# The last strip of a mixture of experts: output rows stored whole, the strip put over them by an indirect store

## The reference

```python
    combine = jnp.einsum('nk,nke->ne', top_w, jax.nn.one_hot(expert_id, N_EXPERTS, dtype=jnp.float32)).astype(xf.dtype)
    y = jnp.zeros_like(xf)
    for e in range(N_EXPERTS):
        h = jax.nn.silu(xf @ w_gate[e]) * (xf @ w_up[e])
        y = y + combine[:, e:e + 1] * (h @ w_down[e])
```

## Time and profile before

| | |
|---|---|
| median of 3 runs | 1213.24 us (1210.46 to 1216.31) |
| the profiled execution | time 1210.47 us, span of its records 1208.6 us |
| mean granted clock of TensorE | 0.978 of full speed |
| TensorE busy | 94% of the span (5834 products) |
| VectorE, ScalarE, POOL busy | 39%, 15%, 4% |
| moved by DMA | 327.6 MB, 271 GB/s over the span |
| chain that ended last | TensorE 80%, VectorE 9%, DMA 6%, ScalarE 4% |

### The profile page before, as it was taken

How to read it: one execution, slowest core, us unless ns; L and a number is a source line. 1 busy time by engine, 2 the same in 40 slices (tenths; PEclk the granted TensorE clock), 3 DMA queues, 4 the chain that set the end, 5 groups by cost and what they waited for, 6 DMA issues and landing times.

```text
span 1208.6 us, 14025 instructions
## 1 busy us (share of the span) xinstructions
PE 1131.5 (94%) x5834; PEld 555.5 (46%) x5834; DVE 471.1 (39%) x966; ACT 186.6 (15%) x401; POOL 48.8 (4%) x63
## 2 busy tenths in 40 slices
PE   7999999999999999999999999999999999959985
PEld 4334343344444455677777673333333333333332
DVE  5000069199565654011123465233333333412332
ACT  2103123200231243000022431000000000000010
POOL 0002000100000012100000001000000000000000
PEclk9999999999999999999999999899999999979998
DMA  8835623655342348854445739999999999999995
GB/s 294 289 129 131 184 86 124 226 174 174 105 137 91 124 184 336 290 145 139 139 158 218 283 116 406 397 415 426 428 426 427 427 425 429 425 427 427 426 427 227
DMA packets 71084, 327.60 MB, mean 271 GB/s; under 512 B 14006, under 2 KB 17878, under 8 KB 54444
## 3 DMA queue, kind: packets, MB, share of 16 engines
q1 hardware_dynamic: 55152, 282.65, 59.8%
q0 software_dynamic: 7888, 37.06, 8.1%
q10 hardware_dynamic: 7980, 6.99, 2.4%
HBM read 318.45 MB, written 10.49 MB: 272 GB/s over the span
## 4 chain that ended last, share of the span: by engine, by line
PE 80%; DVE 9%; DMA 6%; ACT 4%; issue 1%; DVEq 0%; POOL 0%; SPq 0%; ACTq 0%
PE PS L715 21%; PE PS L1042 16%; PE PS L1320 13%; PE PS L1402 7%; DMA ring<-in_w_up 5%; PE PS L1281 4%; PE PS L688 3%; PE PS L1327 2%; DVE X L2087 2%; DVE top L2086 2%; PE PS L1379 1%; PE PS L1285 1%; PE PS L1395 1%; PE PS L709 1%; DMA X<-in_x_prompt 1%
## 5 line engine op out<-in xcount | busy, mean ns | idle before, releaser
L715 PE MATMUL PS<-ring,NC 128*128 128x512 f32 x704 | 320.8, 600 | 1.8 <-issue 1.8
L715 PEld LDWEIGHTS PS<-ring,NC 128*128 128x128 f32 x704 | 128.7, 191 | 153.6 <-issue 152.0
L1042 PE MATMUL PS<-NC,ring 128*128 128x288 f32 x768 | 189.9, 407 | 1.6 <-DVE X L2244 0.5
L1320 PE MATMUL PS<-ring,NC 128*64 128x512 f32 x560 | 163.7, 605 | 7.4 <-DMA ring<-in_w_up 6.8
L1042 PEld LDWEIGHTS PS<-NC,ring 128*128 128x128 f32 x768 | 144.6, 190 | 42.4 <-issue 1.2
L2437 DVE TENSOR_TENSOR X<-X,PS 128x1024 f32<-128x1024 f32 x52 | 63.5, 1221 | 118.9 <-PE PS L1281 118.9
L1320 PEld LDWEIGHTS PS<-ring,NC 128*64 128x64 f32 x560 | 46.3, 138 | 101.3 <-issue 99.9
L1281 PE MATMUL PS<-XNN,NC 64*128 64x512 f32 x208 | 59.1, 645 | 1.4 <-DVE XNN L2475 0.8
L2244 DVE TENSOR_TENSOR X<-X,PS 128x288 f32<-128x288 f32 x16 | 7.3, 455 | 112.0 <-PE PS L1042 112.0
L1931 ACT ACTIVATE NC<-PS,small 64x512 f32<-64x512 f32 x11 | 7.5, 681 | 273.5 <-PE PS L1320 239.7
L1327 PE MATMUL PS<-ring,NC 128*32 128x256 f32 x384 | 36.0, 451 | 14.7 <-DMA ring<-in_w_up 14.7
(11 more groups left out here) (460 smaller groups left out, 1174.0 us busy)
## 6 DMA issues: line engine op xcount, KB each, us to landing
ring<-in_w_gate SPq DMA_DIRECT2D x27, 2048.0 KB, 19.7
ring<-in_w_up SPq DMA_DIRECT2D x22, 2048.0 KB, 17.1
ring<-in_w_in SPq DMA_DIRECT2D x36, 1024.0 KB, 5.1
ring<-in_w_down SPq DMA_DIRECT2D x16, 2048.0 KB, 18.6
ring<-in_w_out SPq DMA_DIRECT2D x16, 1024.0 KB, 5.1
nine<-in_w_down SPq DMA_DIRECT2D x6, 2048.0 KB, 22.0
XNN<-in_w_up SPq DMA_DIRECT2D x5, 2048.0 KB
NC<-in_w_gate SPq DMA_DIRECT2D x5, 2048.0 KB
```

Source lines behind the costliest of these rows:

```text
L715: last = mm(acc(n, t)[:, 0:width], lhs[:, kt, t * 128:(t + 1) * 128], slot(m)[:, k, 0:width], start=kt == 0, stop=kt == KT - 1)
L1042: last = mm(PS[:, j, 0:NT], slot(m)[:, k, 128 * j:128 * j + 128], src[:, kt, :], start=kt == 0, stop=kt == width * 4 - 1)
L1320: last = mm(PS[64 * half:64 * half + 64, 2, :], x[:, kt % 8, kt // 8, :], weights[half][:, kt % 8, :], start=kt == 0, stop=kt == KT - 1)
```

## The change

The last block is combined earlier and the last strip takes another way.

- The combine of block 13 now stands in the gate and up products of expert 15 (`COMBINED_IN`), with strip 0 alone; the rows of strip 1 in `ysb` are cleared by VectorE first. All five steps stand there, and VectorE does their adds before it scales the last hidden. After them, `hx` lacks nothing but the last strip.
- VectorE then signals `rows_final`, and SP stores `hx` as three stores of whole rows.
- TensorE gathers the strip's 32 rows from `hx` by a one-hot matrix `last_hot` (12 products, `last_base`) into bank 5, and the last down product is accumulated on top of them. For this the routing weight is multiplied into the scale of the last hidden.
- VectorE and ScalarE copy the bank into `last_rows`, one instruction each, and POOL writes it over the stored rows by two indirect DMAs, one for the prompt and one for the sample rows, in pieces of 512 columns; rows that belong to the other output are out of bounds and left out. POOL waits for the three stores first.
- The indices and `last_hot` are made by VectorE in the routing.
- The overflow loops of SP, ScalarE and VectorE stand inside `If(nov > 0)`.

```diff
@@ -106,6 +106,7 @@
     put("half", ((p >= 64) + 2 * EMPTY).astype(np.float32))
+    put("quad", (p // 32 + 4 * EMPTY).astype(np.float32))
@@ -410,13 +411,17 @@
         rnk, s32, l32, later = (small[:, 352 + 16 * i:368 + 16 * i] for i in range(4))
         strips = small[:, 416:424].rearrange("p (s b) -> p s b", s=2)
         over_rs = small[:, 490:491]
+        last_tab, last_at, last_out = small[:, 424:427], small[:, 428:429], small[:, 430:431]
+        last_hots = natS[:, 64:256].rearrange("p (i t r) -> p i t r", i=2, t=3)
+        last_hot = last_hots[:, 0, :, :]
+        last_rows = XN[:, 0:512]
+        ids_prompt, ids_sample = ids[:, 114:115], ids[:, 115:116]
         iota_t = gh[:, 0:NT]
         slot_w = C_[:, 3840:3840 + 2 * NT].rearrange("p (b t) -> p b t", b=2)
         NCOMB, NCOMB_OV = 5, 6
         KEYS_WITH_Q = 9
         TOKENS = (0, 128, NT - 128)
         ROW0 = NBK * CAP
-        LAST = [(t, x) for t in range(3) for x in range(2)]
         def sub_of(p):
@@ -438,7 +443,7 @@
             return XT2 if b == BSTAR + 1 else XT
         COMBINED_IN = {p: p - 1 for p in range(1, NFULL)}
-        COMBINED_IN.update({PSTAR: BSTAR - 1, PSTAR + 1: BSTAR, PSTAR + 2: BSTAR + 1})
+        COMBINED_IN.update({PSTAR: BSTAR - 1, PSTAR + 1: BSTAR, PSTAR + 2: BSTAR + 1, NEXP - 1: NBK - 1})
         ids_nov, ids_exp = ids[0:1, 90:91], ids[0:1, 91:91 + NOVF]
         ids_order = ids[0:1, 16:32]
         ids_slot, ids_blk = ids[:, 80:86], ids[:, 108:114]
@@ -454,7 +459,7 @@
         HELD = [(NLOT - 2 + i) % NRING for i in range(2)]
         SPARE = [i for i in range(NRING) if i not in HELD][:NL]
         FREED = NLOT + NRING - 2
-        NCOMB_IN = NCOMB * (NBK - 1)
+        NCOMB_IN = NCOMB * NBK
         r_at = [0]
@@ -558,19 +563,18 @@
             sp.wait_ge(S("route_ready"), 1)
             nov = sp.value_load(ids_nov, min_val=0, max_val=NOVF)
             sp.wait_ge(S("moe_free"), FREED)
-            with sp.Fori(0, NOVF) as b:
...
-            for n, (t, x) in enumerate(LAST):
-                sp.wait_ge(S("y_ready"), n + 1)
-                y, row = (y_prompt, t * 128) if t < 2 else (y_sample, 0)
-                sp.dma_start(bass.AP(y.tensor, row * D + 512 * x, [[D, ROWS[t]], [1024, 2], [1, 512]]),
-                             hx[0:ROWS[t], t, :].rearrange("p (h x c) -> p h x c", h=2, x=2)[:, :, x, :])\
-                    .then_inc(S("y_stored"), 16)
-            sp.wait_ge(S("y_stored"), 16 * len(LAST))
+            with sp.If(nov > 0):
+                with sp.Fori(0, NOVF) as b:
...
+            sp.wait_ge(S("rows_final"), 1)
+            for t in range(3):
+                y = y_prompt[0, t * 128:(t + 1) * 128, :] if t < 2 else y_sample.rearrange("b s d -> (b s) d")
+                sp.dma_start(y, hx[0:ROWS[t], t, :]).then_inc(S("y_stored"), 16)
+            sp.wait_ge(S("y_stored"), 48)
         @block.gpsimd
@@ -644,6 +648,14 @@
                 with pool.If(nov > b):
                     pool.wait_ge(S("xt_ready"), NBK + b)
                     block_rows(NBK + b, 1, "ov_x")
+            pool.wait_ge(S("last_ids"), 1)
+            pool.wait_ge(S("y_stored"), 48)
+            pool.wait_ge(S("last_rows"), 2)
+            for y, at, rows in ((y_prompt[0].rearrange("t (c n) -> (t c) n", c=4), ids_prompt, 4 * T),
+                                (y_sample.rearrange("b s (c n) -> (b s c) n", c=4), ids_sample, 4 * R)):
+                nc.gpsimd.indirect_dma_start(y, bass.IndirectOffsetOnAxis(ap=at, axis=0), last_rows, None,
+                                             bounds_check=rows - 1, oob_is_err=False).then_inc(S("y_put"), 16)
+            pool.wait_ge(S("y_put"), 32)
         @block.tensor
         def _(pe):
@@ -1293,11 +1305,21 @@
                         pe.wait_ge(S("y_out_psum"), k + 1)
                     elif k == BSTAR:
                         pe.wait_ge(S("y_out_psum"), NFULL)
+                    elif k < NBK - 1:
+                        pe.wait_ge(S("y_strips"), 4 * (k - NFULL + 2 - (k > BSTAR)))
                     else:
-                        pe.wait_ge(S("y_strips"), 4 * (k - NFULL + 2 - (k > BSTAR)))
+                        pe.wait_ge(S("y_strips"), 2 * NLIGHT)
                 if NCOMB * k + s:
                     pe.wait_ge(S("comb_free"), NCOMB * k + s)
                 combine(k % 2, s, 6).then_inc(S("comb"), 1)
+
+            def last_base():
+
+                pe.wait_ge(S("last_ids"), 1)
+                for t in range(3):
+                    for c in range(4):
+                        mm(PS[32 * c:32 * c + 32, 5, :], last_hot[0:ROWS[t], t, :], hx[0:ROWS[t], t, 512 * c:512 * c + 512],
+                           start=t == 0, stop=False)
             def combine_over(b, s):
@@ -1373,20 +1395,12 @@
                                   start=True, stop=True)
                 return last
-            def strip_down(bank, w, f):
+            def strip_down(bank, w, f, add=False):
                 for c in range(4):
                     last = mm(PS[32 * c:32 * c + 32, bank, :], hTs[:, f, :], w[:, f % 2, 512 * c:512 * c + 512],
-                              start=f == 0, stop=f == 3)
+                              start=f == 0 and not add, stop=f == 3)
                 return last
-
-            def last_combine(t, x, banks):
-
-                for half in range(2):
-                    rows = slice(64 * half, 64 * half + 64)
-                    last = mm(PS[0:ROWS[t], banks + half, :], slot_w[rows, (NBK - 1) % 2, t * 128:t * 128 + ROWS[t]],
-                              ysb[rows, (NBK - 1) % 2, 512 * x:512 * x + 512], start=True, stop=True)
-                last.then_inc(S("last_comb"), 1)
             def hidden_t(bank=3):
@@ -1423,12 +1437,12 @@
                         last = strip_down(1, w, f)
                     last.then_inc(S("moe_free"), 1)
-            def light_down(bank, landed, done):
+            def light_down(bank, landed, done, add=False):
                 for q in range(2):
                     w = landed(4 + q).rearrange("p (f n) -> p f n", f=2)
                     for f in range(2 * q, 2 * q + 2):
-                        last = strip_down(bank, w, f)
+                        last = strip_down(bank, w, f, add)
                     done(last, q)
@@ -1462,6 +1476,8 @@
                 if p == 0:
                     return tables
+                if p == NEXP - 1:
+                    return lambda s: combine_step(NBK - 1, s)
                 return lambda s: combine_step(COMBINED_IN[p], s) if p in COMBINED_IN and s < 4 else None
             for p in range(NEXP):
                 b, sub = block_of(p), sub_of(p)
@@ -1498,11 +1514,12 @@
                 strip_hidden_t(hid).then_inc(S("ht_ready"), 1)
                 if b + 1 == BSTAR and sub:
                     block_rows_t(BSTAR + 1)
-                if p in COMBINED_IN:
+                if p in COMBINED_IN and p < NEXP - 1:
                     combine_step(COMBINED_IN[p], 4)
                 if p == NEXP - 1:
                     pe.wait_ge(S("route_ready"), 1)
                     pe.wait_ge(S("comb_free"), NCOMB_IN)
+                    last_base()
                     nov = pe.value_load(ids_nov, min_val=0, max_val=NOVF)
                     with pe.If(nov > 0):
                         with pe.Fori(0, NOVF) as o:
@@ -1522,21 +1539,12 @@
                                 for s in range(NCOMB_OV):
                                     combine_over(o, s)
                                 pe.wait_ge(S("comb_free"), o * NCOMB_OV + (NCOMB_IN + NCOMB_OV))
+                        last_base()
                 pe.wait_ge(S("ht_laid"), hidden_of(p))
                 if p < NEXP - 1:
                     light_down(4 + sub, lots_at(p), lambda last, q: last.then_inc(S("moe_free"), 1))
                 else:
-                    light_down(4 + sub, lots_at(p), lambda last, q: last.then_inc(S("y_last"), 1))
-            pe.wait_ge(S("y_strips"), 2 * (NLIGHT + 1))
-            for n, (t, x) in enumerate(LAST[:4]):
-                last_combine(t, x, 2 * n)
-            pe.wait_ge(S("y_ready"), 1)
-            for half in range(2):
-                rows = slice(64 * half, 64 * half + 64)
-                for x in range(2):
-                    last = mm(PS[32 * x:32 * x + 32, half, :], slot_w[rows, (NBK - 1) % 2, T:NT],
-                              ysb[rows, (NBK - 1) % 2, 512 * x:512 * x + 512], start=True, stop=True)
-            last.then_inc(S("last_comb"), 1)
+                    light_down(4 + sub, lots_at(p), lambda last, q: last.then_inc(S("y_last"), 1), add=True)
         @block.scalar
@@ -1970,15 +1978,16 @@
                         strip_rows(b, sub, 4 + sub)
             act.wait_ge(S("route_ready"), 1)
             nov = act.value_load(ids_nov, min_val=0, max_val=NOVF)
-            with act.Fori(0, NOVF) as b:
...
+            with act.If(nov > 0):
+                with act.Fori(0, NOVF) as b:
...
             act.wait_ge(S("y_last"), 2)
-            strip_rows(NBK - 1, 1, 5)
```

(43 more changed lines are left out.)

60 lines of the change are left out of this document (30 added, 30 removed).

## The result

The change makes the kernel slower: 1221.57 us (median of 20 runs, 1214.94 to 1226.35) against 1214.43 (20 runs, 1207.31 to 1222.36), ratio 1.0056 with a 95% interval of 1.0037 to 1.0075. By the ratio that is 6.8 us more, where 2.5 us less were forecast.

The account below looks back on a forecast made before the run. Weight stream bounds the expert stage, leaving a 16.2 us tail. Gate/up +0.6, sample adds +1.0, base +2.85 with clock, 5.8 scatter, against removed copies, combines, adds, stores: -2.5 us, 1213.2 to 1210.7; range 1213.2 - 7 to 1213.2 + 1.5.

Parts of the forecast that it names:

- Step 1: Last strip's gate/up products: five combine steps move in, three free in the weight wait, two costing 2.2 us.
- step 2: Last gate/up products: shorter idle stretch, some 1.5 us, gives full clock; 3.8 + 2.2 = 6.0 us, end at 1188.75.
- rival A: Clock stays low in the second gate/up half and the base: end 1208.0, -0.6 us; chance 0.17.
- Step 3: VectorE's sample-row adds precede the hidden's scaling: adds until 1190.25, scaling until 1190.75, 1.0 us of new wait.
- Step 4: Behind the transposes: base 2.85 us, 32 down instructions 3.8 us, 1.0 us for clock; rows ready at 1200.3.
- Step 5: Three stores, skipped loops costing only a branch: `rows_final` 1191.3, issue 1191.4, landed 1199.8; unskipped loops would hold them 4 us.
- Step 6: POOL's scatters at the end: second starts 1202.3, lands in 3.5 us (bounds 2.6 and 11.3), 0.3 program end: 1206.1.
- Step 7: Free edits: 2.5 us of extra VectorE routing operations and about 1.5 us of strip clears, hidden in existing waits.
- C: Scatter landing in series at the end makes it slower: no gain from 6.0 us, +5.3 us at 11.3; chance 0.12.
- E: Loops not skipped, or stores held by another wait: stores move to 1203.8, end 1209.6, +1.0 us; chance 0.03.

Follow-up runs that it names:

- experiment 1: Kernel after without TensorE's overflow part (count load, branch and body): ratio 1.0005 to the kernel before.
- experiment 2: Kernel after storing only the 32 sample rows, the two stores of prompt rows left out: one execution, 27.4 us from last `up` weights to end.
- experiment 3: Kernel after with SyncE instead of POOL waiting for the two scatters: ratio 1.0034 to the kernel before.
- experiment 4: Kernel after without the two scatters and the wait for them: one execution, 29.1 us from last `up` weights to end.
- experiment 5: Kernel after with TensorE loading the overflow count before the last expert and branching ahead of the base products: ratio 0.9995 to the kernel before.
- experiment 6: As experiment 5, with SyncE waiting for the scatters and the hidden scaled ahead of the sample-row adds: ratio 0.9984 to the kernel before.
- experiment 7: Kernel after with stores written as 2 KB pieces, though data still moved in 8 KB packets: ratio 1.0036 to the kernel before.
- experiment 8: Kernel after without `If(nov > 0)` around the SyncE, ScalarE and VectorE loops: one execution, 30.1 us from last `up` weights to end.
- experiment 9: As experiment 5, with SyncE waiting for the scatters and two thirds of the base products moved into idle time: ratio 0.9984 to the kernel before.
- experiment 10: As experiment 9, with the first two tiles stored as soon as they are final: ratio 0.9979 to the kernel before.
- 9, timed again: The unchanged kernel of experiment 9 timed once more: ratio 0.9975 to the kernel before.

## Why the prediction was wrong

- **Steps 1 and 2** held in the profile of the kernel after, but the clock of step 2 in no other profile in which the base stands whole behind the transposes. The three steps before the second half's weights cost nothing; idle time ahead of it was 1.63 us (forecast 1.5), and products and combine steps ran at full clock: 6.0 us forecast, and the last combine step ended at 1186.66, 5.0 us after the start with 16 products to go. In the profiles of experiments 1 to 8 TensorE had stood 2.67 us for the last `up` weights, and the low clock was there, 1.6 us longer up to the same point (5: 6.6 us), as rival A had it. Why the one profile of the kernel after has the shorter wait is open. In experiments 9 and 10 the wait was 1.5 to 1.7 us and the clock full, and there a third of the base (1.06 us) fills it. So the 31.8 us are a lucky draw: with the low clock, as in experiment 7, the tail is 33.4, 7.4 above the kernel before, where the medians differ by 7.1.
- **Step 3** held to 0.1 us: the second add ended at 1189.1, the scaling at 1189.65. What it did not say is that VectorE's order has no better choice while the stores wait for the same adds (experiment 6).
- **Step 4 failed, and it is the step that carries the loss.** "The 32 down instructions, 3.8 us" took 0.99 + 2.97 + 5.95 = 9.9 us. I followed the branches of VectorE and SyncE and looked at TensorE's only as hidden; I did not ask what it leaves to be fetched, and that the change moves it behind the base products and beside 2.4 MB of stores. Of the 6.1 us too much 2.97 are the stall, the rest the low clock in the products behind it (25 take 3.0 us at full clock); both are gone when the branch is left out (experiment 1) or taken earlier (experiment 5). The base itself took 4.48 us against 2.85 + 1.0. Together with a start one microsecond early this gives copies at 1205.95 instead of 1200.3.
- **Step 5** held in its size: `rows_final` came 1.4 us earlier than forecast and the stores landed at 1199.1, forecast 1199.8, 9.1 us behind their issue instead of 8.4. But its price for the loops was one-sided: skipped, they bring the stores earlier and the stall with them; not skipped, the tail was 1.8 us shorter, and 3.4 shorter than that of experiment 7, which had the same low clock (experiment 8).
- **Step 6**: the scatters landed in 2.5 us in the median, below the chosen 3.5 and just below the lower bound of 2.6, which was not worked out from a row. The 3.3 us taken as fixed were read off a gather that did not have the engines to itself: it was issued at 463.5 and the next one at 465.25. The two scatters also moved 0.16 MB together, not 256 KB each, because the rest was out of bounds. The first was issued 0.98 us behind the copies, forecast 0.7. The 0.3 us for the end of the program was a guess without a row, and POOL's drain takes 2.36 us: 7.4 us from the copies to the end instead of 5.8. Where the Trainium skill's price (DMA: Bandwidth & Descriptors, Anatomy of one DMA; an estimate of 2.6 us for 256 KB) and the gather's row differed, the scatter's own row, 2.5, is close to the page; with so few bytes it bears on the fixed part only.
- **Step 7** held: the new routing operations took 2.4 us of VectorE's wait for the first hidden.
- **The rivals.** C ended on the right side for a wrong reason: the landing, its mechanism, was short. E was nearest in naming a loop or wait, at TensorE none. The mechanism that decided had no rival, and the range ended at 1214.7 where 1221.6 was measured. The kernel before itself came out at 1214.4 over 20 runs instead of the 1213.2 that the range was built on; that 1.2 does not change the picture.

For the fetch the Trainium skill (Runtime: NRT & Kernel Launch, Instruction fetch mechanics) has a sentence that speaks against this change, and I had not weighed it: "A taken branch whose target isn't in the current 2-page window forces a DMA fetch of the target page before execution can continue". The runs agree that a fetch follows this branch, 1.1 us behind it in experiments 2, 5 and 8; they do not show that nothing runs before it, since the first 7 down products behind the branch did. It stalled TensorE by 3.0 to 3.2 us where stores lay ahead of it, by 0.5 and 0.8 where they moved beside it (9, timed again, and 10), and else not.

What stays open: why the fetch comes only when the bytes of the stores are through (in experiment 10, nearly through), and is not let in between them earlier. Experiment 7 was meant to ask whether the size of their packets is the reason and did not change it; another queue or fewer bytes in flight was not tried either.

## What to carry to other kernels

In this kernel the branch that skips a large body was a DMA in disguise: ask when its code is fetched and what stands in the DMA engines then, before moving stores beside it or it beside stores. Take the branch as early as its condition allows, and load the condition earlier still. A chain that ends in a GpSimd transfer pays for the drain of that engine as well, unless another engine waits in its place; and when a new product enters the path, look first for the idle time of the same engine in which its operands are already there.

## What the runs showed of the hardware

- The fetch packet for TensorE's code (16 KB) came 1.1 to 1.2 us behind the branch where at the time of the branch the stores' bytes had not begun to move or were through (before, and experiments 2, 5, 6, 8 and 9), and 4.7 us behind it where 2.4 MB of stores had begun to move 1.5 us ahead of it (after, and experiments 3, 4 and 7). TensorE went on 1.3 to 1.5 us after the end of the packet in all six profiles in which it stood.
- POOL's drain at the end of the program took 2.36 us after a wait, with or without DMAs of its own; started at once behind the last issue it ran 4.36 us beside the landing, and the end came 1.3 us sooner.
- The two scatters into memory, 0.16 MB together, landed in 2.7 and 2.3 us.
- TensorE's clock went to its low level for some 3 us in the base products although 16 transposes ran directly ahead of them (idle time before the transposes: 2.08 us). In experiment 9 that idle time was 1.22 us and the base ran at full clock; in its first profile the low level then came in the down product, in the second not at all.
